# Four unread transposes of a constant between the fp32r products, at nine places of a two-block transformer kernel

## What is computed

```python
def first_block(...):                      # one layer
    x  = x  + 0.5 * ml[2] * swiglu(modulate(rms_norm(x, ...)), ffn1_w_in, ffn1_w_out)
    cx = cx + 0.5 * mc[2] * swiglu(modulate(rms_norm(cx, ...)), ffn1_w_in, ffn1_w_out)
    # projections by w_in; short convolution; q/k norms, rope; attention of x over context and x
    x = x + ml[5] * merge_branches(y_conv, o_attn, gates, w_branch_conv, w_branch_attn, w_out)
    x = x + 0.5 * ml[8] * swiglu(modulate(rms_norm(x, ...)), ffn2_w_in, ffn2_w_out)
    return rms_norm(x, final_g)

def second_block(x, ...):
    x = even_layer(x, ...)   # w_in_ab: gated recurrence (mlstm) and stick-breaking attention, w_out_ab
    x = odd_layer(x, ...)    # w_in_c: four groups pooled over 2, 4, 8, 16 tokens, pool_w, silu gate, w_out_c
    return x

def swiglu(h, w_in, w_out):
    a, b = jnp.split(h @ w_in, 2, axis=-1)
    return (jax.nn.silu(a) * b) @ w_out
```

## Time and profile before

| | |
|---|---|
| three executions | 1361.89, 1363.85 (median), 1367.06 us |
| profiled execution, its own time | 1367.78 us |
| its span, first to last instruction | 1365.3 us |
| TensorE busy | 1323.2 us, 97% |
| VectorE, ScalarE, GpSimd busy | 906.4 (66%), 648.5 (48%), 30.3 us (2%) |
| mean granted TensorE clock | 0.987 |
| DMA | 229.67 MB, 168 GB/s mean |

### The profile page before, as it was taken

One profiled execution on the slowest core, in us unless ns is written; L12 is line 12 of the kernel. 1 busy time (PEld: TensorE's weight loads), 2 busy tenths in 40 slices (PEclk: granted clock), 3 DMA queues, 4 the chain that ended last, 5 costly groups with the idle time before them and its releaser, 6 DMA issues.

```text
span 1365.3 us, 23443 instructions
## 1 busy us (share of the span) xinstructions
PE 1323.2 (97%) x9310; PEld 1214.3 (89%) x9310; DVE 906.4 (66%) x1462; ACT 648.5 (48%) x1025; POOL 30.3 (2%) x29
## 2 busy tenths in 40 slices
PE   5999999999999999999999999999999999999996
PEld 3688888888898889899999999989999999998996
DVE  3577875546558486654775555788886757688853
ACT  3433222223236335554554444666666766555552
POOL 0000000000010000000000000200000001000000
PEclk6999999999999999999999999999999999999998
DMA  8755656555544344444556565556544554355550
GB/s 301 259 168 185 213 195 209 172 199 203 173 134 157 106 124 150 142 140 155 175 155 189 183 192 169 158 163 182 162 148 140 173 167 156 112 161 180 183 168 31
DMA packets 201403, 229.67 MB, mean 168 GB/s; under 512 B 7120, under 2 KB 191696, under 8 KB 201296
## 3 DMA queue, kind: packets, MB, share of 16 engines
q1 hardware_dynamic: 201008, 227.90, 52.7%
q10 hardware_dynamic: 288, 0.29, 0.1%
HBM read 227.11 MB, written 1.05 MB: 167 GB/s over the span
## 4 chain that ended last, share of the span: by engine, by line
PE 85%; DVE 9%; ACT 3%; issue 2%; DMA 1%; SPq 0%; DVEq 0%; ACTq 0%
PE P L1030 25%; PE P L1031 25%; PE P L1032 25%; DVE WL L1855 2%; DVE TS L1783 1%; PE P L1146 1%; PE P L1036 1%; PE P L1038 1%; PE P L1037 1%; PE P L1134 1%; PE P L992 1%; DMA W<-in_w_mod 1%; ACT WH L1450 1%; PE P L1123 1%; PE P L1139 1%
## 5 line engine op out<-in xcount | busy, mean ns | idle before, releaser
L1030 PE MATMUL P<-XHB,WH 128*128 128x256 f32 (+1 forms) x1808 | 562.1, 311 | 11.1 <-DVE TS L1822 4.0
L1031 PE MATMUL P<-XLB,WH 128*128 128x256 f32 (+1 forms) x1808 | 546.6, 302 | 0.0
L1032 PE MATMUL P<-XHB,WL 128*128 128x256 f32 (+1 forms) x1808 | 546.4, 302 | 0.0
L1855 DVE TENSOR_TENSOR WL<-W,WH 128x1024 fp32r<-128x1024 f32 x358 | 431.5, 1223 | 103.7 <-ACT WH L1450 103.4
L1450 ACT ACTIVATE WH<-W 128x1024 fp32r<-128x1024 f32 x358 | 369.0, 1041 | 258.0 <-PE P L1032 180.2
L1030 PEld LDWEIGHTS P<-XHB,WH 128*128 128x128 f32 x1808 | 341.3, 189 | 39.1 <-issue 18.4
L1031 PEld LDWEIGHTS P<-XLB,WH 128*128 128x128 f32 x1808 | 341.2, 189 | 17.9 <-issue 3.1
L1032 PEld LDWEIGHTS P<-XHB,WL 128*128 128x128 f32 x1808 | 343.0, 190 | 14.9
L1030 PE MATMUL P<-GH,WH 128*128 128x256 f32 (+1 forms) x372 | 122.0, 328 | 0.0
L1031 PE MATMUL P<-GL,WH 128*128 128x256 f32 (+1 forms) x372 | 121.5, 326 | 0.0
L1032 PE MATMUL P<-GH,WL 128*128 128x256 f32 (+1 forms) x372 | 121.5, 326 | 0.0
(11 more groups left out here) (302 smaller groups left out, 1814.3 us busy)
## 6 DMA issues: line engine op xcount, KB each, us to landing
W<-in_ffn_w_in SPq DMA_DIRECT2D x88, 512.0 KB, 4.7
W<-in_w_in_ab SPq DMA_DIRECT2D x72, 512.0 KB, 4.5
W<-in_w_modt SPq DMA_DIRECT2D x56, 512.0 KB, 3.9
W<-in_w_in SPq DMA_DIRECT2D x52, 512.0 KB, 3.6
W<-in_ffn_w_out SPq DMA_DIRECT2D x40, 512.0 KB, 4.6
W<-in_w_in_c SPq DMA_DIRECT2D x32, 512.0 KB, 4.1
W<-in_w_mod SPq DMA_DIRECT2D x16, 512.0 KB, 6.9
W<-in_w_out_ab SPq DMA_DIRECT2D x16, 512.0 KB, 4.4
```

The lines of the kernel that those rows point to most:

```text
L1030: pe.matmul(o, h[:, k, c], xh[:, kk, a:b], start=kk == 0, stop=False)
L1031: pe.matmul(o, h[:, k, c], xl[:, kk, a:b], start=False, stop=False)
L1032: mm = pe.matmul(o, l[:, k, c], xh[:, kk, a:b], start=False, stop=kk == gm.nk - 1)
L1855: dve.tensor_tensor(l, a, h.bitcast(F32), ALU.subtract).then_inc(S["wl"], 1)
```

## The change

A new step `settle` is put behind nine calls: behind the first and the third `ma`, behind the pairs `fa2`/`fb2` of blocks 0, 6 and 12, behind the first `oz` of groups 1 and 3, and behind the first two calls of `p1`. (The short description of the change speaks of ten places; the program has nine.) Each does four 128x128 transposes of the constant of ones into a side bank that nothing reads. The step waits for the reader of that bank's last content, and does not take the bank from the turn.

```diff
+    def settle(self):
+
+        b = 4 + self.uses % 3
+        self.step("settle", bank=b, free=self.bank_free.get(b))
...
             self.gemm("ma", i, w["w_branch_attn"], 0, 8, 256 * i, (0, T), first=i == 0)
+            if i in (0, 2):
+                self.call(self.settle)
...
                     self.gemm("oz", i, WC, 0, 8, 2048 + 512 * g + 256 * i, LAT, g=g)
+                if g in (1, 3) and i == 0:
+                    self.call(self.settle)
...
             self.gemm("p1", i, w["w_out_c_2"], 0, 16, 256 * i, (0, T), first=i == 0, norm=i == 3)
+            if i < 2:
+                self.call(self.settle)
...
                 self.gemm(f"fb{n}", f, win, 0, 8, DFF + f * 128, cols)
+                if n == 2 and f in (0, 6, 12):
+                    self.call(self.settle)
...
+                elif s.kind == "settle":
+                    for c in range(4):
+                        pe.transpose(ps[:, c * 128:c * 128 + 128], con("one"), con("id"))
```

## The result

| | before | changed |
|---|---|---|
| executions | 22 | 22 |
| median | 1363.41 us | 1371.63 us |
| lowest, highest | 1359.34, 1369.56 us | 1362.71, 1373.81 us |
| ratio of the changed to before | | 1.0045, 95% interval 1.0029 to 1.0060 |
| profiled execution, its own time | 1367.78 us | 1363.50 us |

What follows compares the result with a forecast made beforehand. TensorE, busy in 97% of the span, was taken as the bound through when its products start. Terms 0.52 + 5.21 + 0.70 - 0.23 = 6.2 us, off the profiled 1367.78 us, gave 1361.6 us; range 1356 to 1368 us.

Steps and rivals of the forecast that it cites:

- The bound and the two pitches: Whole kernel: TensorE's product starts set the time, 256-token products starting 117.8 (long) or 113.3 ns (short) apart, 4.44 ns difference.
- The cost of one place: At each place of four transposes: 0.46 us where the pitch comes out short, 0.44 us where it stays long.
- The FFN's term: Second FFN: 1482 products turned short behind block 0 save 6.59 us, less three places, 1.38: a gain of 5.21 us.
- the change copies just them: The attention's transposes, 16 times in the trace, serve as precedent: 10 of 14 long pitches turned short, 2 of 2 short kept.
- Group 1 of the odd layer: Odd layer, group 1: pitch already short, nothing gained; the place costs between 0.46 us and nothing, taken as 0.23 us.
- Group 3 and the output projection: Odd layer's group 3 and output projection: 468 products turned short save 2.08 us, less three places, 1.38: gain 0.70 us.
- Behind the attention: After the attention's last gather: 324 products turned short save 1.44 us, less two places, 0.92: gain 0.52 us.
- The executions against the profiled one: Before's spread comes from FFNs drawn long or short, worth 6.8 us; the change should bring all executions near 1361.6 us.
- The transposes do not turn the pitch: Rival, second FFN: pitch stays long behind the transposes, nine places at 0.44 us cost 4.0 us, giving 1371.7 us; chance 0.10.
- the rule with the 192 ns load: Long pitch at the attention's transposes: which weight load lasts 192 ns seems to tell what turns; the FFN's line 1032 turned three times.

## Why the prediction was wrong

- **The bound and the two pitches.** Right in the main. TensorE's starts set the time, 117.8 and 113.3 ns occur in every trace, the granted clock was 1.00 over the FFN behind block 0 at either pitch, and 4.44 ns by the number of products is the largest part of the differences between the profiled executions. There are not only two values: in the trace of before 84 products from 390.36 to 400.43 us, behind products of 512 columns, start 119.9 ns apart at a granted clock of 1.00.
- **The cost of one place, 0.46 us.** Right. It closes the account of the 12.3 us.
- **The FFN's term, "1482 x 4.44 ns = 6.59 us", gained.** This is the step that failed. It holds in the first profiled execution of the changed kernel only, and by luck: the FFN opened long of kind 0 there, not of the kind 2 that I had argued from. In the two further profiles of all nine places the FFN opened short with 278 ns, which I had not known as a phase of its own, and the first place made it long; the 6.6 us came on top, not off. The time of 20 of the 22 executions fits that. It would also fit an FFN that opens long of kind 1 and is left so, as in the profile of the FFN's places alone; none of the three profiles of the nine shows that, and the other 21 executions have no trace.
- **What I took as proof.** I counted 16 `turn` steps and read a rule from which load lasts 192 ns: the FFN's kind, line 1032, had turned three times of three. In eleven of the later traces that kind stayed long at 55 `turn` steps, five in each; the last product ahead lasted 282 ns there, and 283 at all 24 where it turned. My three cases were one case met three times, since the attention repeats itself. "Of the 2 that met the short pitch both kept it" was true of `turn` steps and is so in every trace; one of the two even had the 278 ns that matter. What failed there is "the change copies just them": four transposes of the constant behind 278 ns gave long 14 times of 14.
- **Group 1 of the odd layer, "0.23 us".** Wrong: I priced the place and left out what it can do to a short pitch. The place made 430 short products long in all three profiles of the nine, 1.9 us.
- **Group 3 and the output projection, 0.70 us.** Right in two of the three profiles, with the pitch short behind all three places. In the first profile the place in group 3 left a long pitch of kind 2 (last product 286 ns), and 192 of the 468 products stayed long.
- **Behind the attention, 0.52 us.** Half right. The first place turned the stretch short in seven of seven profiles; the second, where it had four transposes, turned it back in four of four. One place would have earned 1.0 us, two earned 0.4 less 0.9.
- **The executions against the profiled one.** Right: before draws its FFN long or short, and the second profile shows a short one. The conclusion that the change brings all executions near 1361.6 us was wrong; most come out near 1371.5 us, which fits the long pitch.
- **The rivals.** "The transposes do not turn the pitch" gave 1371.7 us, and 1371.63 was measured. That the numbers agree is luck, and the mechanism is half right: I had the FFN open long and stay so, with nine places at 0.44 us on top of the profiled execution. In the two profiles that went long it opened short and was made long. I gave it 0.10, on the strength of the rule with the 192 ns load. The gap that the Trainium skill (TensorE: Matmul & The Clock Gate, Back-to-back issue gap) gives for a product by itself, 109 ns for 256 columns, is not the pitch of any stretch of such products here; 113.3 ns is the shortest.

The prediction asked how likely a draw is, and should have asked what the state is that the transposes act on. Long or short is too coarse a state.

## What to carry to other kernels

A small instruction put in to shift a stream's rhythm acts on a phase, and its effect can be of either sign in the next execution; one profile before and one after can both be the rare case, so look at the spread of the executions first and profile the common one. Repeats of a loop body are one precedent, not many. Nor is one kind of small instruction a precedent for another. Where a rhythm is worth having, find a sequence that ends in it from every phase that occurs (here four, then three), not one that ended in it where you looked; here it took back the loss and no more.

## What the runs showed of the hardware

- Streams of fp32r products of 256 columns at a granted clock of 1.00 have two stable pitches, 113.3 and 117.8 ns, each kept over up to 1541 products without a gap. A third, 119.9 ns, was seen for 84 products behind products of 512 columns.
- What follows a group of transposes of the constant went by the phase ahead of it and the number of transposes, in the four common phases without exception, with 112 places in the cells of the table that hold more than one. The phase shows in single ns of a product or a load. The attention's own transposes do not follow that table: behind a short pitch with 278 ns four of them gave short 28 times of 28, where four of the constant gave long 14 times of 14.
- A phase outlives other engines' work in part: the places behind `ma` change what the FFN's first place meets some 47 us later, behind a norm that runs over ScalarE and VectorE. With all nine places 20 of 22 executions took 1366 us or more; without those two 12 executions took 1363.29 to 1371.19 us. Why is open. Whether the phase lies between the stream of loads and that of products, as the 192 ns load suggests, is argued only.
